# Scaling x on VectorE and summing the modulation's first quarter on TensorE at the start of a two-block transformer kernel

## The reference, cut to what matters

```
cond = jax.nn.silu(c)
mod = cond @ w_ada[l] + b_ada[l]
shift, scale, gate = jnp.split(mod, 3, axis=-1)
h = rms_norm(x, norm_g[l]) * (1.0 + scale[:, None, :]) + shift[:, None, :]
proj = h @ w_in[l]
...
def rms_norm(x, g):
    xf = x.astype(jnp.float32)
    xf = xf * lax.rsqrt(jnp.mean(xf * xf, axis=-1, keepdims=True) + EPS)
    return (xf * g.astype(jnp.float32)).astype(x.dtype)
```

## Time and profile before

| | us |
|---|---|
| median of 3 runs | 1308.66 (1308.22 to 1310.09) |
| the profiled execution | 1308.78 |
| its span, first to last instruction | 1307.0 |
| PE busy | 1276.8 (98%) |
| PE weight loads | 919.8 (70%) |
| DVE busy | 936.8 (72%) |
| ACT busy | 380.1 (29%) |
| POOL busy | 277.2 (21%) |

### The profile page before, as it was taken

The page is one execution under the profiler, slowest core; times in us unless marked ns, Lnnn a source line. Parts: engine busy times, 40 slices in busy tenths (PEclk is TensorE's granted clock), DMA queues, the critical chain, the costliest instruction groups (busy, mean ns, idle before and its releaser), DMA issues.

```text
span 1307.0 us, 17546 instructions
## 1 busy us (share of the span) xinstructions
PE 1276.8 (98%) x6256; PEld 919.8 (70%) x6256; DVE 936.8 (72%) x2147; ACT 380.1 (29%) x942; POOL 277.2 (21%) x264
## 2 busy tenths in 40 slices
PE   4999999999999999999999999999999999999998
PEld 3444455544788876875455556888888888888887
DVE  5898999768786896564556676676867777786563
ACT  4223121226411112223456675110232232220000
POOL 1168577315003668600000000001000000000000
PEclk9999999999999999999999999999999999999999
DMA  9793423660412141202111003113223233233210
GB/s 318 196 157 105 150 52 120 187 210 24 161 41 78 65 127 67 67 31 98 65 32 35 1 2 65 65 69 109 65 82 113 65 99 95 65 116 126 92 46 33
DMA packets 91041, 120.67 MB, mean 92 GB/s; under 512 B 16488, under 2 KB 52654, under 8 KB 90956
## 3 DMA queue, kind: packets, MB, share of 16 engines
q1 hardware_dynamic: 86256, 110.81, 28.2%
q10 hardware_dynamic: 2956, 5.05, 1.2%
q0 software_dynamic: 1744, 3.70, 1.0%
HBM read 111.00 MB, written 6.84 MB: 90 GB/s over the span
## 4 chain that ended last, share of the span: by engine, by line
PE 87%; DVE 8%; ACT 2%; issue 1%; DMA 1%; ACTq 0%; DVEq 0%
PE bank L1583 18%; PE bank L1609 10%; PE bank L934 8%; PE bank L921 8%; PE bank L1511 7%; PE bank L1244 6%; PE bank L1469 6%; PE bank L956 6%; PE bank L1349 4%; PE bank L1421 3%; PE bank L1449 3%; PE bank L1554 2%; PE bank L985 1%; PE bank L1200 1%; PE bank L1091 1%
## 5 line engine op out<-in xcount | busy, mean ns | idle before, releaser
L1583 PE MATMUL bank<-arena 128*128 128x256 f32 x1120 | 241.9, 379 | 0.0
L1583 PEld LDWEIGHTS bank<-arena 128*128 128x128 f32 x1120 | 212.8, 190 | 28.9
L1609 PE MATMUL bank<-arena 128*128 128x256 f32 x616 | 133.1, 379 | 0.0
L1609 PEld LDWEIGHTS bank<-arena 128*128 128x128 f32 x616 | 117.0, 190 | 15.9
L934 PE MATMUL bank<-arena 128*128 128x512 f32 x288 | 127.7, 596 | 0.0
L956 PEld LDWEIGHTS bank<-arena 128*128 128x128 f32 (+2 forms) x660 | 77.8, 143 | 70.8 <-issue 46.9
L1244 PE MATMUL bank<-arena 128*128 128x256 f32 x560 | 122.4, 380 | 0.0
L1244 PEld LDWEIGHTS bank<-arena 128*128 128x128 f32 x560 | 106.0, 190 | 15.1 <-issue 0.7
L956 PE MATMUL bank<-arena 128*128 128x128 f32 (+2 forms) x660 | 92.3, 278 | 21.4 <-ACT arena L1693 7.8
L3168 DVE CUSTOM_DVE_ANT_0 arena<-bank,arena 128x128 f32<-128x128 f32 (+3 forms) x128 | 57.5, 488 | 66.0 <-PE bank L1421 64.7
L921 PE MATMUL bank<-arena 128*128 128x512 f32 (+1 forms) x256 | 102.2, 552 | 0.0
(11 more groups left out here) (399 smaller groups left out, 2010.3 us busy)
## 6 DMA issues: line engine op xcount, KB each, us to landing
arena<-in_w_in SPq DMA_DIRECT2D x14, 2048.0 KB, 7.8
arena<-in_w_up SPq DMA_DIRECT2D x20, 1024.0 KB, 6.9
arena<-in_w_ada SPq DMA_DIRECT2D x16, 512.0 KB, 8.8
arena<-in_w_down SPq DMA_DIRECT2D x8, 1024.0 KB, 7.4
arena<-in_w_out SPq DMA_DIRECT2D x2, 2048.0 KB, 9.7
arena<-in_w_attn_br SPq DMA_DIRECT2D x8, 512.0 KB, 7.6
arena<-in_w_o SPq DMA_DIRECT2D x2, 2048.0 KB, 8.6
rb_dram<-rb_one_dram ACTq DMA_DIRECT2D x1, 2560.0 KB
```

The lines of the kernel that those rows point to most:

```text
L1583: mm = pe.matmul(ps, left[:, k, :], right[:, k, :], start=(first and k == 0), stop=(k == 3), skip_group_check=True)
L1609: mm = pe.matmul(down_acc(i, name), left, right, start=first and name in ("P1", "P7", "P2", "P4"), stop=last, skip_group_check=True)
```

## The change

- Line 90: a new tile `silw`, 128 x 8 x 32. DVE clears it and writes silu(c) into column 0 of each of the eight blocks.
- PE gets `mod_rows`, between `x_turns` and `mod_turn(0)`: eight matmuls, block k of silw (32 columns) against block k of the first quarter of w_ada (512 columns), into the 32 partitions of bank 2 that begin at 32 * (k % 4). Blocks 4 to 7 add onto blocks 0 to 3. Row 0 of each strip then holds a partial sum of the modulation, the other rows zero.
- DVE copies this bank to macc[0] in place of `mod_sums(0)`; `mod_turn(0)` sums it over the partitions as before. `mod_sums(1)` to `(3)` stay.
- ACT no longer scales x, and copies lam behind the squares. DVE scales each tile of x as its root comes, ahead of exp.
- The new name "msum" takes bank 2 and raises the count of helper names by one, so all later helper tiles without a bank of their own stand one bank further on.

```
+        silw = arena[:, BASE + 6144:BASE + 6400].rearrange("p (k n) -> p k n", k=KT)
...
         name_aux(*[("x", k) for k in range(KT)])
+        name_aux("msum", banks=2)
         name_aux(("mod", 0), banks=3)
...
+            def mod_rows():
+
+                ps = begin_aux("msum")
+                pe.wait_ge(silc_done, 1)
+                for k in range(KT):
+                    if k % 4 == 0:
+                        pe.wait_ge(ada_in[0][k // 4], 32)
+                    c = 32 * (k % 4)
+                    mm = pe.matmul(ps[c:c + 32, :], silw[:, k, :], adaS[0][:, k, :], start=(k < 4), stop=(k >= 4),
+                                   skip_group_check=True)
+                mm.then_inc(aux_done, 1)
...
             x_turns("x", xrow, (xn_done, TT))
+            mod_rows()
             pe.wait_ge(pool_ones, 1)
             mod_turn(0)
...
-            aux_ready(act, "lam")
-            act.activation(sp[:, 2:4, :], abank("lam")[:, 0:64].rearrange("p (a b) -> p a b", a=2), ACT.Copy)\
-               .then_inc(afree("lam"), 1)
             for t in range(TT):
                 act.wait_ge(x_in[t], 16)
                 if t:
                     act.wait_ge(sq_done, t)
                 act.activation(sqx, xrow[:, t, :], ACT.Square, accum_out=stat[:, t:t + 1]).then_inc(sq_done, 1)
-            for t in range(TT):
-                act.wait_ge(root_done, t + 1)
-                act.activation(xrow[:, t, :], xrow[:, t, :], ACT.Copy, scale=stat[:, t:t + 1]).then_inc(xn_done, 1)
+            aux_ready(act, "lam")
+            act.activation(sp[:, 2:4, :], abank("lam")[:, 0:64].rearrange("p (a b) -> p a b", a=2), ACT.Copy)\
+               .then_inc(afree("lam"), 1)
...
-            v.tensor_scalar(silc[:, 0:8], silc[:, 0:8], 0.5, None, ALU.mult).then_inc(silc_done, 1)
+            step(v.memset(silw, 0.0))
+            v.tensor_scalar(silw[:, :, 0], silc[:, 0:8], 0.5, None, ALU.mult)
+            step(v.tensor_scalar(silc[:, 0:8], silc[:, 0:8], 0.5, None, ALU.mult))
+            v.sem_inc(silc_done, 1)
...
-            aux_out(v, "lam")
+            for t in range(TT):
+                v.wait_ge(root_done, t + 1)
+                v.tensor_scalar(xrow[:, t, :], xrow[:, t, :], stat[:, t:t + 1], None, ALU.mult).then_inc(xn_done, 1)
             v.wait_ge(ldt_in, 16)
             exp_(t_(DT), t_(LDT))
+            aux_out(v, "lam")
             mul(t_(XR), t_(LR), t_(DT))
             mul(t_(TH), t_(LI), t_(DT))
-            mod_sums(0)
+            aux_ready(v, "msum")
+            v.tensor_copy(macc[0], abank("msum")[:, :]).then_inc(macc_done, 1)
+            v.wait_ge(macc_done, 1)
+            v.sem_inc(afree("msum"), 1)
```

## The result

The changed kernel is slower: 1314.18 us in the median of 11 runs (1312.48 to 1317.91), against 1310.09 of the kernel before in the same session. The ratio is 1.0036, 95% interval 1.0027 to 1.0045: 3.5 to 5.9 us more. The profiled execution took 1312.72 with a span of 1310.9, so 3.9 us more than the one before. The forecast was 1308.8 and 1307.4 to 1311.3.

The account below looks back on a forecast made before the run. TensorE was taken as the bound, busy 1276.8 of 1307.0 us. Square -0.7, scaling -2.25, mod_rows +1.9, copy +0.8 and small instructions +0.3 summed to 0.0 us: forecast 1308.8, range 1307.4 to 1311.3.

Parts of the forecast that it names:

- lam behind the squares, last root: ACT's squares of x: fourth square at 12.1 in place of 12.79, 0.7 us won; last root's power done at 14.15.
- Scaling on DVE: Each tile of x scaled as its root comes, 0.75 us for the fourth; turns start at 15.2, counted as -2.25 us.
- The collision: DVE's scaling of tile 2 over POOL's two instructions of tile 3: 0.25 us added, between 0 and 0.45.
- x_turns now the same 5.18: PE's turns of x: from their start to the column sums 5.18 us as before, so over at 20.4.
- rival C: Clock at the turns of x: all run at the low level, 7.0 us not 5.3, +1.7 us, 1310.4; chance 0.15.
- mod_rows 1.9: Eight new 32x512 matmuls on PE behind the turns, four column strips at once: 1.9 us, between 1.87 and 6.93.
- Rivals A and B: At mod_rows: A, strips don't overlap, 5.0 us, 1313.8, chance 0.13; B, half overlap, +2.0 us, 1310.8, chance 0.11.
- Copy and small instructions: On DVE behind mod_rows: bank copy with signals 0.8 us, then six small instructions 1.3 us, ahead of mod_cols(0).
- mod_cols(0) at 24.4: DVE's step that everything behind passes through: starts at 24.4 us against 24.39 before, shift 0.0 us.
- The shift reaches the end in full; behind it PE is full: Behind mod_cols(0): any shift of its start reaches the end in full; PE waits only 0.16 us at 84.27.
- "I count nothing" for the banks: Banks of all later helper tiles move on by one: no cost counted, 0.3 us either way.
- D: Rival at the scaling: DVE and POOL collide at all four tiles, x not scaled earlier, +1.3 at most, 1310.0; chance 0.04.

Follow-up runs that it names:

- e12: Kernel before with one 128x512 filler matmul, its result unread, in PE's gap ahead of the first projection: 1309.46 us, ratio 0.9996.
- e8: Kernel before with two 128x512 filler matmuls on PE between the turns of x and the column sums: 1315.35 us, ratio 1.0041.
- e4: Changed kernel with every later helper tile in its bank of before, "msum" left out of the count: 1314.39 us, ratio 1.0037.
- e10: Changed kernel, sums between sixth and seventh turn, six small DVE instructions before the copy, one filler before the projection, 22 one-element matmuls in PE's first waits: 1310.78 us.
- e11: e10 without the 22 one-element matmuls in PE's first waits: 1311.26 us, ratio 1.0011.
- e13: Changed kernel with 22 one-element matmuls on PE while it waits for its first loads: 1313.18 us, ratio 1.0031.
- e15: Kernel before with 22 one-element matmuls on PE while it waits for its first loads: 1311.45 us, ratio 1.0016.
- e1: Kernel before with only lam behind the squares and x scaled on DVE; first-quarter sums stay on DVE, behind exp: 1313.16 us, ratio 1.0032.
- e2: Kernel before with only the first-quarter sums moved to PE; lam and scaling on ACT as before: 1314.02 us, ratio 1.0036.
- e3: Changed kernel with PE's two gaps around mod_turn(0) filled by matmuls nobody reads ("the filled gaps"): 1310.88 us, ratio 1.0016.
- e5: Kernel before with 11 small 128x32 matmuls on PE ahead of the turns of x: 1309.93 us, ratio 1.0008.
- e17: e10 without the filler before the projection, but with two 128x128 filler matmuls in the gap at 291.6 us: 1311.27 us, ratio 1.0013.

## Why the prediction was wrong

By its own steps:

- *lam behind the squares, last root.* Right in kind. The fourth square started at 12.26 (forecast 12.1). When x lands differs by 0.9 us among executions: in the six kernels with ACT's order as before the fourth square started between 11.85 and 12.79, and in the twelve with lam behind the squares between 11.62 and 12.46. The kernel before had been profiled with the latest start of all, so the 0.7 us forecast here were for the most part the draw: the means of the two groups are 0.2 us apart.
- *Scaling on DVE.* 0.75 us, right. The collision was there, on the other side: POOL's first instruction took 0.54 beside DVE's scaling of the tile before, and 0.31 a tile earlier. Turns at 15.52; forecast 15.2, range to 15.4.
- *x_turns now the same 5.18.* 6.1 us, 0.9 more, the first term of the sum that was mis-sized. Part of rival C: the turns went at the slow pace longer, with transposes of 417 ns until 20.3 us, 4.8 us behind their start, where it had been 3.2. The same turns took 5.05 to 6.63 us in all these kernels, also where nothing near them was changed (e12, e8). The granted clock reads 1.00 over both paces. I didn't find what sets it.
- *mod_rows 1.9.* 1.92. Rivals A and B, 0.24 of the chance, are refuted: four column strips over the same rows run at once, 3.6 times as fast as the 6.93 us of eight untiled. The Trainium skill ("TensorE: Matmul & The Clock Gate", "The mechanism") has weight loads overlap matmuls in flight only where the row groups differ. This trace does not agree, since all four strips have the same rows; the measurement decides.
- *Copy and small instructions.* From the end of mod_rows (23.54) to 25.85 they took 2.3 us; forecast 2.1. Nearly right.
- *mod_cols(0) at 24.4.* 25.85: 0.3 from the start, 0.9 from the turns, 0.2 from the rest.
- *The shift reaches the end in full; behind it PE is full.* This is the step that failed. 1.46 us of shift became 2.6 at 84 us and 3.9 at the end. I counted each wait that moved and never asked what the new waits of PE do to its clock, which I had at nothing without a reason. Behind them twelve projection records took 7.08 us in place of 5.39. My own order of steps had a gap in it: PE idle from the end of mod_rows through signal, copy and signal, right ahead of the 1.3 us gap that was there. Before, the sums were over while PE turned x, and PE ran on. Rival C had the clock, but at the turns alone and at 1.7 us.
- *"I count nothing" for the banks.* Right about the banks (e4), wrong about the rest: there was a cost far behind that I had no term for. Eight matmuls more on PE (sixteen records) move an instruction packet in among the packets of a load, 0.8 to 0.9 us at 528, and bring a stall of PE by 290 us, 0.4.
- *The rivals' times.* By their own terms C is 1310.5 and not 1310.4, and D, 4 x 0.45 less the 0.25 that the forecast had, is +1.55 and 1310.4, not 1310.0. Neither moves the range.

The sum in hindsight, for the profiled pair: front +1.46, clock behind it +1.1, the stall +0.4, the late load +0.8; that is 3.8 of 3.9. The padding agrees in size, with 0.75 us (e10 against e11) and 0.85 (e13 against changed) between spans of clock 0.999. The filled gaps take 2.8 us away in the medians, more than one fall costs here; the changed kernel's many executions at 0.996 are the likely reason, which no trace of it shows. That the medians are 4.1 us apart and this pair of traces 3.9 is partly luck: the profiled before is a late execution by some 1.0 us, and the profiled changed kernel is one of the better four.

What stays open: what sets the pace of the turns, why the clock gives way at 56 to 68 us without a gap, why it falls in a gap in one execution and not in another, what the stall of 0.4 us waits for (only its going with the length of PE's program was seen), and the time outside the span in e15. That the instruction packet is PE's is inferred from its moving with the number of PE's instructions and not with DVE's, which e1 changed.

## What to carry to other kernels

When work moves from an engine that ran in another's shadow onto that other, count the new round trip (end, signal, copy, signal) as idle time of the moved-to engine, ask what its clock does behind it, and put something independent between the producer and its reader, here the last two turns. Where a stretch that you didn't touch gets slower at a fixed place, look at the granted clock there and at the DMA view for an instruction packet, before looking for a new wait. And a gain of a microsecond at the beginning is smaller than what the clock takes or leaves elsewhere: compare offsets place by place, and many runs.

## What the runs showed of the hardware that I had not expected

**A code block among a load's packets.** In the 18 traces the time from the issue of the 2 MB load to its first use had one of two values. With the instruction packet 3.9 to 5.7 us behind the issue it was 8.8 to 9.1 us (changed, e2, e3, e4, e5, e11); with the packet 6.8 to 7.0 behind it, or ahead of it, 7.7 to 7.9 (all others). The packet, from the DMA view of the changed kernel at 521 to 522 us: kind, packets, MB, share of 16 engines in 1 us.

```profile
q1 hardware_dynamic: 197, 0.40, 104.8%
q8 instruction: 1, 0.02, 6.6%
```

6.6% of 16 engines for 1 us is one DMA engine for 1.05 us, which is the delay of the load and the length of its end on one engine. The Trainium skill ("Runtime: NRT & Kernel Launch", "Instruction fetch mechanics") says that each engine's code is refilled in blocks of 16 KiB over its own DMA queue and that the cost is mostly hidden. The size fits: the profile before has 51 such packets of 0.84 MB in all, 16.5 KB each. In this trace PE has no wait of its own from 516 to 528 us, but a load was late that DVE waits for, and PE waits for DVE.

**The clock fell behind two waits of 1.0 and 1.5 us** in four traces of four, and behind a single one of 1.3 in one of six. It also fell with no wait at all, at 56 to 68 us. By 84 us the falls cost between 0.7 us (e2) and some 3.6 (the second of e17), and the clock was low for 3.4 us in the changed kernel and for 10.2 in e17's second.

**Small fp32 matmuls are not all cheap**: in PE's first waits 128x32 with a 128x128 weight took 0.44 us each, one element with one column of weights 0.06. The 0.44 is at the slow pace of the first turns: on the full clock at 255 us even 128x64 with a 128x128 weight took 0.22. Which part of the difference is the weights' was not measured.
